# A hybrid decoder trunk on one Trainium2 core: attention and gate steps re-laid between the levels of a triangular inverse

## What is computed

```
proj = h @ w_in                                   # fox q,k,v; pool; gdn q,k,v; z; gates
# A: forgetting attention, 8 heads x 64, queries in blocks of 128
s = einsum('bqhd,bkhd->bhqk', qi, k) * scale + ci[..., None] - cum_k
pr = softmax(where(causal, s, -inf)); branch_a = einsum('bhqk,bkhd->bqhd', pr, v)
# C: gated DeltaNet, 4 heads x 128, chunks of 64
L = einsum('bhnid,bhnjd->bhnij', k_beta, k) * decay(tri_strict)
T = triangular_solve(eye + L, eye); u = T @ v_beta; w = T @ (k_beta * exp(g))
v_new = u_c - w_c @ state                         # scan over 4 chunks
o = (q_c * exp(g_c)) @ state + a_c @ v_new
state = state * exp(gl) + k_dec^T @ v_new
o = o * rsqrt(mean(o * o) + eps) * norm_g * silu(z)
merged = sum(sigmoid(gates) * (branches @ w_branch)); h = LayerNorm(alpha*h + merged @ w_out)
```

## Time and profile before

| | us |
|---|---|
| median of 3 runs (lowest, highest) | 1946.81 (1946.05, 1950.1) |
| the profiled execution | 1946.16 |
| its span | 1944.4 |
| TensorE busy in the span | 1743.2 |
| VectorE, ScalarE, GpSimd busy | 1385.4, 915.4, 683.1 |

### The profile page before, as it was taken

The page is one execution under the profiler, slowest core; times in us unless marked ns, Lnnn a source line. Parts: engine busy times, 40 slices in busy tenths (PEclk is TensorE's granted clock), DMA queues, the critical chain, the costliest instruction groups (busy, mean ns, idle before and its releaser), DMA issues.

```text
span 1944.4 us, 26703 instructions
## 1 busy us (share of the span) xinstructions
PE 1743.2 (90%) x7280; PEld 1018.2 (52%) x7280; DVE 1385.4 (71%) x3865; ACT 915.4 (47%) x2233; POOL 683.1 (35%) x583
## 2 busy tenths in 40 slices
PE   8999999999999878878799999999999998877776
PEld 7987887544444223223289778875454442322222
DVE  5775577977777777776468745679777787777764
ACT  5555452444445444444455555424444454544443
POOL 0100002454443465655301100024444444566553
PEclk9999999999999999999999999999999999999999
DMA  6533479999999999999945335899999999999997
GB/s 241 169 115 89 150 273 367 414 426 427 426 427 396 423 427 427 428 427 427 406 146 171 99 98 153 295 367 408 427 426 427 427 402 424 420 428 427 427 427 305
DMA packets 106731, 660.63 MB, mean 340 GB/s; under 512 B 11888, under 2 KB 12288, under 8 KB 40064
## 3 DMA queue, kind: packets, MB, share of 16 engines
q0 software_dynamic: 75376, 546.57, 67.3%
q1 hardware_dynamic: 31248, 112.74, 17.4%
HBM read 658.20 MB, written 1.06 MB: 339 GB/s over the span
## 4 chain that ended last, share of the span: by engine, by line
PE 31%; issue 24%; DMA 23%; DVE 13%; ACT 7%; POOL 1%; DVEq 1%; ACTq 0%; POOLq 0%; SPq 0%
PE acc L746 11%; DMA arena<-experts_dram,idxu 10%; DMA cst<-experts_dram,stage 8%; DMA arena<-experts_dram,stage 4%; PE acc L765 3%; DVE arena L1527 3%; PE psum L697 2%; DVE arena L1583 2%; PE psum L729 2%; PE psum L666 2%; PE psum L667 2%; PE psum L668 2%; DVE arena L1373 1%; ACT w_hi_r L1084 1%; PE acc L666 1%
## 5 line engine op out<-in xcount | busy, mean ns | idle before, releaser
L765 PE MATMUL acc<-arena 128*128 128x512 f32 x896 | 439.5, 619 | 119.6 <-ACT arena L1187 119.2
L746 PE MATMUL acc<-arena 128*128 128x512 f32 x896 | 412.2, 601 | 27.9 <-ACT arena L1161 27.8
L632 POOL DMA_INDIRECT arena<-experts_dram,stage x224 | 312.3, 1394 | 218.3 <-PE acc L765 167.5
L1557 DVE CUSTOM_DVE_ANT_0 arena<-arena,h 128x1024 f32<-128x1024 f32 x224 | 274.6, 1226 | 137.0 <-issue 59.7
L765 PEld LDWEIGHTS acc<-arena 128*128 128x128 f32 x896 | 157.3, 193 | 400.1 <-issue 399.9
L614 POOL DMA_INDIRECT arena<-experts_dram,idxu x224 | 247.5, 1105 | 304.5 <-PE acc L746 276.0
L1527 DVE CUSTOM_DVE_ANT_0 arena<-arena,h 128x1024 f32<-128x1024 f32 x224 | 274.7, 1226 | 105.8 <-DMA arena<-experts_dram,idxu 102.0
L746 PEld LDWEIGHTS acc<-arena 128*128 128x128 f32 x896 | 163.2, 190 | 255.7 <-issue 152.0
L1434 DVE TENSOR_TENSOR raw_r<-raw,w_hi_r 128x1024 fp32r<-128x1024 f32 x152 | 180.2, 1221 | 81.6 <-ACT w_hi_r L1084 80.8
L1181 ACT ACTIVATE gel<-dots 128x1 f32<-128x1 f32 x256 | 51.7, 202 | 296.0 <-DVE dots L1557 295.5
L1084 ACT ACTIVATE w_hi_r<-raw 128x1024 fp32r<-128x1024 f32 x152 | 154.1, 1052 | 61.6 <-DMA raw<-weights_dram 56.6
(11 more groups left out here) (295 smaller groups left out, 2763.1 us busy)
## 6 DMA issues: line engine op xcount, KB each, us to landing
raw<-weights_dram SPq DMA_DIRECT2D x168, 512.0 KB, 3.6
arena<-weights_dram SPq DMA_DIRECT2D x20, 512.0 KB, 6.5
w_hi<-weights_dram SPq DMA_DIRECT2D x12, 512.0 KB, 6.6
lnr<-lnrows_dram POOLq DMA_DIRECT2D x4, 1024.0 KB, 6.5
arena<-experts_dram,idxu POOLq DMA_INDIRECT x224, 13.2
arena<-experts_dram,stage POOLq DMA_INDIRECT x224, 13.5
lnr<-cum_dram POOLq DMA_DIRECT2D x2, 1024.0 KB, 9.1
cst<-weights_dram SPq DMA_DIRECT2D x4, 512.0 KB, 5.5
```

The lines of the kernel that those rows point to most:

```text
L632: nc.gpsimd.indirect_dma_start(slots[i % RING][:, :], None, experts[:, :], bass.IndirectOffsetOnAxis(stage[:, i:i + 1], 0)).then_inc(slot_ ...
L746: last = mm(acc[:, c * 512:(c + 1) * 512], diag[:, i % 4, :], slots[n % RING][:, D + c * 512:D + (c + 1) * 512], start=n == 0, stop=n == R ...
L765: last = mm(acc[:, c * 512:(c + 1) * 512], diag[:, i % 4, :], slots[i % RING][:, D + c * 512:D + (c + 1) * 512], start=False, stop=ends)
L1557: nc.vector.tensor_tensor_reduce(slots[i % RING][:, 0:D], slots[i % RING][:, 0:D], h[:, b, :], 1.0, 0.0, ALU.mult, ALU.add, dots[:, i:i + ...
```

## The change

- Attention steps are called by a number `k` from 0 to 7 (block and pair of heads): `attend(k)` lays `fo` of `k-3`, `pt` of `k-2` and `fs` of `k`.
- `wide` pieces get a block index: a step is half a piece (6 matmuls, one token block). The second half of the first gate, before a `gate` step in PSUM banks, becomes a third `wide` group, so there are 24 halves, laid by `gated`. `wide_out` goes by halves, and for the third group takes the Sigmoid at once.
- Shares are normalised ahead of the transposes: at its `pt` step VectorE takes the reciprocal of the sums and scales `fE` in place, and TensorE's `pt` waits for `shares_ready` in place of `fexp_ready`.
- `fo` has the values stationary and the shares moving, and writes its output transposed, 64 rows per head; it is split into `brT` directly. `foT` and the buffer `fo` go.
- The exponentials of the decay move from `gbc` to just ahead of `t4`; two weight splits move one step later.
- `late` stands between `vn(0,1)` and `o(0,1)`, before it stood ahead of `vn(0,0)`.

```diff
@@ steps()
-    s += [("lt", 0), ("at", 0), ("lt", 1), ("at", 1), ("wide", 0, 0), ("t0", 0), ("t0", 1)]
+    s += [("lt", 0), ("at", 0), ("lt", 1), ("at", 1), ("wide", 0, 0, 0), ("wide", 0, 0, 1), ("t0", 0), ("t0", 1)]
...
+    halves = [("wide", i, j, b) for i in range(3) for j in range(4) for b in range(2)][2:]
+    def gated(n):
+        out = []
+        for step in [halves.pop(0) for _ in range(n)]:
+            out += [step] + ([("wide_out", step[1], step[3])] if step[2] == 3 and step[1] < 2 else [])
+        return out
+    def attend(k):
+        out = [("fo", *divmod(k - 3, 4))] if k >= 3 else []
+        out += [("pt", *divmod(k - 2, 4))] if 2 <= k < 10 else []
+        return out + (fs(*divmod(k, 4)) if k < 8 else [])
+
     for lev in range(1, LEVELS):
...
+        s += [("y", lev, c) for c in range(2)] + attend(lev - 1) + gated(1)
+        s += [(k, lev, c) for k in (("ty", "uy") if lev < LEVELS - 1 else ("uy",)) for c in range(2)] + gated(2)
+    s += [("wT", 0), ("wT", 1)] + attend(5) + gated(1)
+    s += [("vn", 0, 0)] + attend(6) + gated(1) + [("o", 0, 0), ("dS", 0, 0)] + gated(1)
+    s += [("vn", 0, 1)] + attend(7) + [("late",), ("o", 0, 1), ("dS", 0, 1)] + gated(1)
+    s += [("vn", 1, 0), ("onorm", 0)] + attend(8) + gated(1) + [("o", 1, 0), ("dS", 1, 0)] + gated(1)
+    s += [("vn", 1, 1)] + attend(9) + [("o", 1, 1), ("onorm", 1)] + gated(1) + [("wide_out", 2, 0), ("wide_out", 2, 1)] + attend(10)
+    for group in gate(1) + br(0) + br(1) + [gate(2)[0], [("oT", 0), ("oT", 1)], gate(2)[1]]:
+        s += group
@@ dense_splits
         if not lo and st[0] == ("gdn", 2, 0):
-            steps = (("gbc", 0), ("gbc", 0), st[0], st[0])
+            steps = (("gbc", 0), ("gbc", 0), st[1], st[1])
@@ TensorE
                     elif kind == "pt":
-                        pe.wait_ge(fexp_ready, 2 * (L * 8 + b * 4 + hp + 1))
+                        pe.wait_ge(shares_ready, L * 8 + b * 4 + hp + 1)
...
-                        for j in range(2):
-                            hd = 2 * hp + j
-                            for kb in range(b + 1):
+                        for kb in range(b + 1):
+                            for j in range(2):
+                                hd = 2 * hp + j
                                 col = (j * (b + 1) + kb) * P
-                                last = mm(ps[:, j * FD:(j + 1) * FD], fP[:, hp % 2, col:col + P], fv[:, kb, hd * FD:(hd + 1) * FD], start=kb == 0, stop=kb == b)
-                    elif kind == "foT":
...
+                                last = mm(ps[j * FD:(j + 1) * FD, 0:P], fv[:, kb, hd * FD:(hd + 1) * FD], fP[:, hp % 2, col:col + P], start=kb == 0, stop=kb == b)
@@ ScalarE
+                    if step == ("t4", 0, 0):
+                        for b in range(NB):
+                            act.wait_ge(*drained(L, ("gbc", b)))
+                            AC(DT[:, b, :], DT[:, b, :], ACT.Exp).then_inc(dt_ready, 1)
+                            AC(egl[:, b, :], glast[:, b, :], ACT.Exp).then_inc(dt_ready, 1)
...
+                        elif kind == "fo":
+                            last = AC(hi, ps[:, 0:P], ACT.Copy)
@@ VectorE
+                        elif kind == "fo":
+                            last = TT(lo, ps[:, 0:P], hi.bitcast(F32), ALU.subtract)
...
-                    elif kind == "fo":
+                    elif kind == "pt":
                         _, b, hp = step
+                        w = (b + 1) * P
                         dve.wait_ge(fexp_ready, 2 * (L * 8 + b * 4 + hp + 1))
                         link(nc.vector.reciprocal(frs[:, b, 2 * hp:2 * hp + 2], fsum[:, b, 2 * hp:2 * hp + 2]))
...
+                        for j in range(2):
+                            hd = 2 * hp + j
+                            last = TS(fE[:, hp % 2, j, 0:w], fE[:, hp % 2, j, 0:w], frs[:, b, hd:hd + 1], None, ALU.mult)
+                        last.then_inc(shares_ready, 1)
```

More of the change, by code:

```diff
@@ L122, in steps @@
-    fill += [gate(0)[1], [("pt", 1, 3), ("fo", 1, 2)], [("fo", 1, 3)], [("foT", 1)]]
-    fill += gate(1) + br(0) + [[]] + br(1) + [gate(2)[0], [("oT", 0), ("oT", 1)], gate(2)[1]]
-    s += fill[0]
-    for i in range(max(len(chain), len(fill) - 1)):
-        s += chain[i] if i < len(chain) else []
-        s += fill[i + 1] if i + 1 < len(fill) else []
+    halves = [("wide", i, j, b) for i in range(3) for j in range(4) for b in range(2)][2:]
[4 more added lines that the diff above has]
+        return out
@@ L527, in split_target @@
             b = step[1]
-            return [brT[:, 1 if kind == "foT" else 0, i, :, b * P:(b + 1) * P] for i in range(2)]
+            if kind == "fo":
+                return [brT[:, 1, i, step[2], b * P:(b + 1) * P] for i in range(2)]
+            return [brT[:, 0, i, :, b * P:(b + 1) * P] for i in range(2)]
         block = ctx.enter_context(nc.Block())
@@ L796, in _ @@
                     if kind == "wide":
[L797 removed]
+                        _, i, j, b = step
                         if j == 0 and i:
[L799 to L800 removed]
+                            pe.wait_ge(wide_drained, NB * (3 * L + i - 1) + b + 1)
+                        gate_piece(L, GROUP_OF["wide", i, 0, 0], j, acc[:, b * 512:(b + 1) * 512], b)
                         if j == 3:
[L802 removed]
+                            ends[b].then_inc(wide_filled, 1)
                         continue
@@ L1805 @@
         w = w_in[L]
-        for step, start in zip((("pool", 0), ("gdn", 0, 0), ("gdn", 1, 0), ("gdn", 2, 0), ("wide", 0, 0), ("fq", 0), ("fk", 0), ("fv", 0)), columns):
+        for step, start in zip((("pool", 0), ("gdn", 0, 0), ("gdn", 1, 0), ("gdn", 2, 0), ("wide", 0, 0, 0), ("fq", 0), ("fk", 0), ("fv", 0)), columns):
             put(step, w[:, start:start + BW], step[0] in ("gdn", "fq", "fk"))
```

77 lines of the change are left out of this document (25 added, 52 removed).

## The result

| | before | after |
|---|---|---|
| median, us (lowest to highest of 5) | 1949.27 (1946.05 to 1950.1) | 1990.42 (1985.71 to 1993.52) |
| profiled execution, its span | 1946.16, 1944.4 | 1990.42, 1988.6 |
| mean granted clock of the span | 0.990 | 0.973 |
| stretch from 0 us to the first transpose of the new `h` (`h1T`), layer 0 | 308.3 | 330.1 |
| the same stretch in layer 1 (from the end of layer 0) | 304.5 | 327.9 |

The changed kernel takes 1.0208 times as long, with an interval of 1.0196 to 1.022. The two stretches of the last rows are the dense stage in which the change lies: they are 21.8 and 23.4 us longer, 45.2 together, which is the whole difference of the spans (44.2). The rest, the expert rows above all, is 1.0 us shorter over both layers.

The account below looks back on a forecast made before the run. TensorE bounds the dense stage: 1946.2 + 2 x 22.1 (new waits) - 2 x 6.3 (waits gone) - 7.2 (decay) - 2 x 1.4 (work) + 2 x 6 (clock) = 1979.8, say 1980 us; range 1948 to 1997.

Parts of the forecast that it names:

- mechanism A: `fo` before `pt` on VectorE and `late` on ScalarE make TensorE wait; 1980 us, chance 0.74.
- Waits that go: TensorE's waits of 2.3 us for `Ym`, 1.9 and 0.6 in attention, and 1.5 of clock loss go; -6.3 us per layer.
- Decay exponentials: Moved exponentials and splits end TensorE's waits for weight rests and `fk` drains; -7.2 us for both layers.
- Less TensorE work: On TensorE, no `foT` -0.8, faster `fo` -1.8, more entries and exits +1.2; sum -1.4 us per layer.
- Six waits at `pt`: TensorE waits for shares while its `fo` passes through ScalarE and VectorE; four at 2.2, two at 1.7, 12.2 us per layer.
- `late` and `onorm`: Per layer, `vn(1,0)` waits 4.7 us for the `o` copy behind `late`; `pt(1,2)` waits 4.6 us behind `onorm(0)`.
- The 0.6 us at `vn(0,1)`: `vn(0,1)` waits for ScalarE's copy of the preceding `o` to free its PSUM bank; 0.6 us per layer.
- Clock: Four of six new waits each bring a clock drop of 1.5 us; +6 us per layer, between 0 and 9.
- The signs that the prediction named: Per layer, six `pt` waits near 2 us, two near 4.6, none for `Ym`, two ScalarE table loads fewer.
- Rival B: ScalarE and VectorE run far enough ahead to hide the new waits; 1923.6 us, chance 0.14 with its mild form.
- C: Only `late` and `onorm` bite, queued TensorE work covers the six short waits; 1943.4 us, 1949 with clock, chance 0.07.
- D: The weight ring starves in one block of weight work; 3 us per layer on top, near 1986 us, chance 0.05.

Follow-up runs that it names:

- kernel 4: The kernel before with only the decay exponentials moved ahead of `t4` and two weight splits one step later; 1940.63 us, ratio 0.9956.
- kernel 3: The changed kernel with `pt` laid ahead of `fo`, and `late` and both `onorm` behind the last half gate piece; 1945.7 us, ratio 0.9985.
- kernel 5: kernel 3 with the second half gate piece moved from ahead of `t0` to between `t0` and the first `y`; ratio 0.9978.
- kernel 10: kernel 5 with the last attention step laid ahead of `late` and both `onorm`; 1950.16 us, ratio 1.0017.
- kernel 1: The changed kernel with `pt` laid ahead of `fo` in each attention step; 1968.74 us, ratio 1.0102.
- kernel 2: The changed kernel, `fo` still ahead of `pt`, with `late` and both `onorm` behind the last half gate piece; 1983.38 us, ratio 1.0156.
- kernel 8: The changed kernel with the old attention output form, `late` and both `onorm` behind the last half piece, one half piece behind `t0`; ratio 1.0107.

## Why the prediction was right, and where its terms were off

The forecast was 1980 us, slower, by mechanism A. Measured 1990.4, inside the range. By its own steps:

- **Waits that go.** Right: the 2.3, 1.9 and 0.6 us are gone. But the prediction left out the first `y`: the whole piece that stood between `t0` and `y` has moved behind `y`, and 1.4 us is new there.
- **Decay exponentials.** 7.2 forecast; the dense work behind them starts 3.0 us earlier in layer 0 (first `wide` matmul at 115.53 instead of 118.50), and kernel 4 measured 5.7 us in the profile and 7.7 in the medians. The size held; in the changed kernel the two waits for `fk` did not go: 0.6 us in layer 0 became 1.2, and 1.7 in layer 1 became 1.3.
- **Less TensorE work: not shown.** The pace taken for `fo` from `lt` and `at` held: its 48 records are busy for 4.4 to 4.6 us in kernels 3, 5 and 10, where the earlier trace rows has 6.5, so 1.9 to 2.1 less of the 2.4 of the better bound. But the term as a whole, -1.4 us a layer, did not arrive. Kernels 3 and 4 differ in form and layout alone. The stages of kernel 3 are 1.5 and 2.3 us longer, with 3.2 and 4.7 us more of idle time and at most 1.7 and 2.6 us less lost to the lower clock, so the work is within 0.3 us the same: what `fo` and `foT` save, the smaller steps around them take.
- **Six waits at `pt`.** Forecast 2.2 four times and 1.7 twice, 12.2 us; measured 2.23 and 2.23 (levels 4 and 5), 2.08 (`wT`), 1.61, 1.53 and 1.53, 11.2 us. The one behind `vn(0,0)`, 1.61, had been put with the long ones. The cause is shown by kernel 1, which changes the place of `fo` and nothing else: 1.0102 instead of 1.0208, some 21 us. Only at level 4 is it not the whole cause, as 2.1 us stay there behind a weight rest.
- **`late` and `onorm`.** 4.7 and 4.6 forecast, 2.40 and 3.85 measured. They are 4.6 and 4.7 in kernel 1, where TensorE isn't late itself: right by their working, but not added to the others. The 0.6 us at `vn(0,1)` did not come.
- **Clock: the term that was mis-sized.** The prediction took four waits of six at 1.5 us, +6 us a layer within 0 to 9, because the two drops it had seen each followed a wait of about 2 us. With the drops that were to go (3.0 and 1.6 us) its clock adds 7.4 us over both layers, its waits 29.0 and its work -2.8: 33.6. Measured over the two dense stages: TensorE idles 13.5 and 11.0 us longer, 24.5. At the lower level it is busy for 27.4 and 40.4 us, before for 6.8 and 8.8, which is at most 26.1 us lost. The stages are 45.2 us longer, so if the work is unchanged, as kernels 3 and 4 have it, the clock took 20.7. Its term was too small by 13 to 19 us and the waits too large by 4.5.

The mechanism was right, and the number is inside the range, but part of its closeness is luck: the errors of the clock and of the waits have opposite signs, and 10 us are left in the total. The signs that the prediction named came with other sizes: six waits between 1.5 and 2.3 us where it said near 2, the two near 4.6 shorter, and three table loads of ScalarE fewer per layer (12 instead of 15) where it had two.

Rival B (waits hidden) is out by the rows of `pt`, C by the six short waits, D by the waits at the weight line, which has none from 100 to 300 us in layer 0. By an estimate, kernel 3 without its last 8.1 us of waits in each layer would take 1945.7 - 16.2 = 1929.5 us, near the 1923.6 of B; no run reached it.

The Trainium skill, page "ScalarE: Activation LUTs", What ACT_TABLE_LOAD costs, was weighed against a row in the prediction, and the trace after decides again: from the accumulator read that ends at 198.53 to the Silu at 199.84 there are 1.31 us, the 1.28 of the load and nothing for a drain. The page's 1.38 us on top does not show.

## What to carry to other kernels

When a product moves from after a step to before it, look at what stands ahead of it on the engine that makes it, not at how early its inputs are: here the exponentials were ready, and the shares stood behind the rest of a copy that had only just been asked for. A new order must be read on each engine's list, with the splits and copies that hang on each step; a step that looks like free cover on TensorE brings work of its own to the others. And price a row of short waits by the clock that the trace grants around them, not by their sum alone: here the clock took about as much as the waits (20.7 to 26.1 us against 24.5). The part of a stretch at the lower level in which the engine idles anyway costs nothing more.

## What the runs showed of the hardware

The clock did not follow the sum of the idle time. Kernels 2 and 8 both have 15.5 us of waits from 100 to 300 us. In kernel 2 they are nine between 1.4 and 2.2 us; in kernel 8 one of 11.3, one of 2.0 and a few below 1.1. The row of kernel 2, then that of kernel 8:

```profile
100.00:300.00 200.00, 184.49 (x1327) 146.01 (x1326) 111.03 (x180) 93.04 (x156) 6.90 (x9) 0.91 0.38 124
```

```profile
100.00:300.00 200.00, 184.37 (x1385) 149.62 (x1383) 117.00 (x176) 97.58 (x156) 6.94 (x9) 0.97 0.44 141
```

0.91 against 0.97, and a stage 10.1 us longer. What counts is the work done at the lower level: TensorE is busy there for 34.5 us in kernel 2 and for 6.2 in kernel 8. The clock of kernel 8 falls within its long wait, from 208.6 to 218.8 us, but the wait lasts until 216.08 and covers most of that stretch. Layer 1 has the same picture, 24.8 us against 7.6. The two kernels also differ in the form of the attention output and in one half piece, so the shape of the waits is the likely cause and not an isolated one. Before the drops of kernel 2 TensorE had been at small matmuls and half gate pieces with a wait of 1.4 to 2.2 us every 9 to 16 us from 149 to 238 us. The Trainium skill, page "TensorE: Matmul & The Clock Gate", A second HAM failure mode: psum-queue depth-cycling, tells of a kernel in which frequent short idles between groups of matmuls were enough to make the clock go back and forth between its two levels; the trace agrees, with no idle above 2.2 us in kernel 2. Its advice in the section HAM oscillation looks at long idles alone, and by that kernel 8 would be the one to lose more; its clock did fall with the long wait, but the measurement has the larger loss in kernel 2.

The clock also differs from one execution, and one layer, to the next with the same waits (0.91 and 0.95 in the two layers of kernel 2). The four executions of kernel 2 lie 12.0 us apart, the four each of kernels 1 and 4 3.9 and 4.2; what decides between them is not shown.
